# Layer A: the last rotated product of two query blocks side by side in halves of TensorE's rows

## The reference, cut to what matters

```
q = concat([q[..., :MLA_NOPE], apply_rope(q[..., MLA_NOPE:], cos, sin)])     # 128 + 64
k = concat([k[..., :MLA_NOPE], apply_rope(k[..., MLA_NOPE:], cos, sin)])     # 128 + 64
s = jnp.einsum('bqhd,bkhd->bhqk', q_blk, k).astype(jnp.float32) * scale
p = jax.nn.softmax(s, axis=-1)
o = jnp.einsum('bhqk,bkhd->bqhd', p, v)
```

## Time and profile before

| | |
|---|---|
| median of 3 runs | 1351.1 us (1350.52 to 1354.14) |
| the profiled execution, its own time | 1349.92 us |
| its span in the trace | 1348.1 us |
| PE busy | 1339.7 us, 99% of the span |
| PEld busy | 1163.8 us, 86% |
| DVE, ACT, POOL busy | 66%, 50%, 29% |
| granted TensorE clock | full in all slices |

### The profile page before, as it was taken

The page is one execution under the profiler, slowest core; times in us unless marked ns, Lnnn a source line. Parts: engine busy times, 40 slices in busy tenths (PEclk is TensorE's granted clock), DMA queues, the critical chain, the costliest instruction groups (busy, mean ns, idle before and its releaser), DMA issues.

```text
span 1348.1 us, 20503 instructions
## 1 busy us (share of the span) xinstructions
PE 1339.7 (99%) x7160; PEld 1163.8 (86%) x7160; DVE 890.7 (66%) x1811; ACT 678.0 (50%) x1544; POOL 395.3 (29%) x511
## 2 busy tenths in 40 slices
PE   9999999999999999999999999999999999999999
PEld 7889888888888889988888898888888888899887
DVE  6776688878796757888582524767766634267871
ACT  6554466545565546777451413545444323157760
POOL 0421251330011323846202213423300122337560
PEclk9999999999999999999999999999999999999999
DMA  8958745334779797541875545333144652654325
GB/s 313 333 211 287 254 145 172 129 137 136 253 240 397 264 360 264 201 151 47 319 259 189 180 157 181 106 110 95 49 150 155 203 174 80 217 178 151 103 75 187
DMA packets 111926, 256.59 MB, mean 190 GB/s; under 512 B 11344, under 2 KB 49104, under 8 KB 111824
## 3 DMA queue, kind: packets, MB, share of 16 engines
q1 hardware_dynamic: 106352, 247.58, 53.0%
q10 hardware_dynamic: 5472, 7.69, 1.8%
HBM read 167.15 MB, written 88.08 MB: 189 GB/s over the span
## 4 chain that ended last, share of the span: by engine, by line
PE 89%; DVE 4%; ACT 2%; DMA 2%; issue 1%; POOL 1%; SPq 0%; ACTq 0%; DVEq 0%; POOLq 0%
PE bank L2057 25%; PE bank L2059 25%; PE bank L2058 25%; PE bank L2102 8%; PE bank L2415 3%; PE bank L2063 2%; PE bank L2064 2%; DMA w_raw<-in_w_mem 1%; DVE w_split L1269 1%; ACT prob L886 1%; DVE probT L1281 1%; DMA w_raw<-in_w_a 0%; DMA w_split<-kept_w 0%; DVE prob L1789 0%; ACT w_split L849 0%
## 5 line engine op out<-in xcount | busy, mean ns | idle before, releaser
L2057 PE MATMUL bank<-actT,w_split 128*128 128x512 f32 x544 | 214.9, 395 | 0.0
L2059 PE MATMUL bank<-actT,w_split 128*128 128x512 f32 x544 | 212.2, 390 | 0.0
L1928 POOL TENSOR_TENSOR prob<-prob,rinv 128x256 f32<-128x256 f32 x192 | 131.0, 714 | 247.8 <-DVE rinv L1443 247.8
L1269 DVE TENSOR_TENSOR w_split<-w_raw,w_split 128x512 fp32r<-128x512 f32 (+3 forms) x204 | 142.0, 708 | 81.6 <-ACT w_split L849 78.9
L849 ACT ACTIVATE w_split<-w_raw 128x512 fp32r<-128x512 f32 (+3 forms) x204 | 122.3, 607 | 126.6 <-DMA kept_w<-w_split 57.8
L2057 PE MATMUL bank<-w_split,actT 128*128 128x512 f32 (+3 forms) x512 | 171.2, 334 | 0.8 <-DMA w_split<-kept_w 0.4
L2058 PE MATMUL bank<-w_split,actT 128*128 128x512 f32 (+3 forms) x512 | 170.2, 332 | 0.0
L2059 PE MATMUL bank<-w_split,actT 128*128 128x512 f32 (+3 forms) x512 | 170.2, 332 | 0.0
L2058 PE MATMUL bank<-actT,w_split 128*128 128x512 f32 x384 | 149.9, 390 | 0.0
L1281 DVE TENSOR_TENSOR probT<-bank,probT 128x512 fp32r<-128x512 f32 (+1 forms) x192 | 112.1, 639 | 21.7 <-ACT probT L859 19.5
L868 ACT ACTIVATE sq<-bank 128x512 f32<-128x512 f32 (+4 forms) x128 | 60.4, 480 | 129.9 <-PE bank L2059 123.1
(11 more groups left out here) (197 smaller groups left out, 3065.3 us busy)
## 6 DMA issues: line engine op xcount, KB each, us to landing
w_split<-kept_w SPq DMA_DIRECT2D x120, 512.0 KB, 4.0
kept_w<-w_split SPq DMA_DIRECT2D x104, 512.0 KB, 5.6
w_raw<-in_w_mem SPq DMA_DIRECT2D x64, 256.0 KB, 3.4
kept_w<-part_split SPq DMA_DIRECT2D x32, 512.0 KB, 5.0
part_split<-kept_w SPq DMA_DIRECT2D x30, 512.0 KB, 4.1
w_raw<-in_w_b SPq DMA_DIRECT2D x44, 256.0 KB, 5.0
w_raw<-in_w_out SPq DMA_DIRECT2D x38, 256.0 KB, 4.5
w_raw<-in_w_a SPq DMA_DIRECT2D x32, 256.0 KB, 4.7
```

Of the source, the lines that this page charges most:

```text
L1269: dve.tensor_tensor(halves(n)[1], w_raw[:, RAW_AT[n] % RAW, 0:width], halves(n)[0].bitcast(fp32), ALU.subtract).then_inc(w_lo_dve, 1)
L1928: pool.tensor_tensor(t, t, rinv[:, par, i:i + 1].to_broadcast(list(t.shape)), ALU.mult).then_inc(p_pool, 1)
L2057: nc.tensor.matmul(out, lhs[0], rhs[0], start=start, stop=False, skip_group_check=skip)
L2059: return nc.tensor.matmul(out, lhs[1], rhs[0], start=False, stop=stop, skip_group_check=skip)
```

## The change

`krT[:, 1, s, :]` now holds the lo part of the rotated key in both halves: DVE writes it twice, and the two memsets go. A new view `q_other[p]`, 256 columns of a row of `actT` that is unused at that time, gets from ACT the hi part of the rotated query of the odd blocks (1 and 3) for both heads of the pair, each in the half in which `qT` has the lo part. The second matmul of `mm2` is taken out of each block's five. Instead, behind the fourth matmul of block 1 and of block 3, two matmuls stand over 64 rows each: that of the block before, from `qT` and `krT` in `half(s)`, and that of the block itself, from `q_other` and `krT` in the other half. They write two different banks.

```diff
+        q_other = [actT[:, 2 * p + 1, 0:2 * P].rearrange("p (b n) -> p b n", b=2) for p in range(PAIRS)]
...
+            def odd_blocks(t):
+
+                return t.rearrange("p (i b n) -> p i b n", i=2, b=2)[:, :, 1, :]
...
                                 hi(("aT", L, p, 4), qT[half(j), 2, j, :], bank(("aT", L, p, 4))[half(j), :], first=j == 0)
+                                hi(("aT", L, p, 4), q_other[p][half(1 - j)], odd_blocks(bank(("aT", L, p, 4))[half(j), :]), first=False)
...
-                for s in range(2):
-                    dve.memset(krT[half(1 - s), 1, s, :].bitcast(fp32), 0.0)
...
                                 lo(("aT", L, p, 4), qT[half(1 - j), 2, j, :], bank(("aT", L, p, 4))[half(j), :],
-                                   qT[half(j), 2, j, :], last=j == 1)
-                                ins = lo(("aT", L, p, 5), krT[half(j), 1, j, :], bank(("aT", L, p, 5))[half(j), :],
-                                         krT[half(j), 0, j, :], last=j == 1, ahead=1)
+                                   qT[half(j), 2, j, :], last=j == 1, ahead=1)
                                 count("hi")
+                                lo(("aT", L, p, 5), krT[half(j), 1, j, :], bank(("aT", L, p, 5))[half(j), :],
+                                   krT[half(j), 0, j, :], last=False, ahead=1)
+                                ins = lo(("aT", L, p, 5), krT[half(1 - j), 1, j, :], bank(("aT", L, p, 5))[half(j), :],
+                                         krT[half(1 - j), 0, j, :], last=j == 1)
                                 if j == 0:
                                     ins.then_inc(first_head, 1)
...
                                 mm3(bank(use)[:], tuple(qT[:, s, a, i * P:(i + 1) * P] for a in range(2)),
                                     tuple(kT[:, a, s, :] for a in range(2)), True, False)
-                                mm2(bank(use)[:], qT[:, 2, s, i * P:(i + 1) * P],
-                                    tuple(krT[:, a, s, :] for a in range(2)), False).then_inc(full(use)[0], 1)
+                                nc.tensor.matmul(bank(use)[:], qT[:, 2, s, i * P:(i + 1) * P], krT[:, 0, s, :], start=False, stop=False)
+                                if i % 2 == 1:
+                                    before = ("aS", L, h, i - 1)
+                                    nc.tensor.matmul(bank(before)[:], qT[half(s), 2, s, (i - 1) * P:i * P], krT[half(s), 1, s, :],
+                                                     start=False, stop=True).then_inc(full(before)[0], 1)
+                                    nc.tensor.matmul(bank(use)[:], q_other[p][half(1 - s), i // 2, :], krT[half(1 - s), 1, s, :],
+                                                     start=False, stop=True).then_inc(full(use)[0], 1)
```

## The result

The changed kernel takes 1359.29 us (median of 5 runs, 1357.87 to 1361.6) where before took 1350.52 us beside it: ratio 1.0062, interval 1.005 to 1.0073. It is slower by 8.8 us by the medians and 8.4 by the ratio. I had forecast 1345.9 us, with 1358 as the end of the range.

What follows compares the result with a forecast made beforehand. The prediction took PE's queue of matmuls to bound the kernel: 5.7 us gained by 32 pairs, less 0.5 us of one softmax wait, takes 1351.1 to 1345.9 us, with a range of 1343.8 to 1358 us.

Steps and rivals of the forecast that it cites:

- What bounds the kernel: Whole kernel: PE, busy 99%, runs a queue of matmuls, so a cheaper matmul shortens the kernel by that much.
- The pair's own price: Layer A's 32 pairs: two overlapping products cost about 240 ns, for two weight loads, where they cost 454 before.
- The changes of rows: Borders of each pair, 128 to 64 rows and back: 35 ns for both changes, pair 275 ns, gain 5.7 us.
- the rival that I gave 0.25: Pair borders: array emptied at each change, up to 162 ns, 64 times; 1355.1 us; chance 0.25 for slower by over 0.3%.
- its form with exposed loads: Pair borders: weight load not hidden either, 118 ns more each change, pair 800 ns, 1362.7 us; chance 0.1 of the 0.25.
- `first_head`: First pair of each layer A: DVE's second key write still ends 0.26 us before PE's first scores load; no wait.
- The banks: Banks of the transposed tiles: PE comes to each over 1 us after it is read, added instructions counted; no wait.
- DVE becomes late: Layer A: DVE's added 11 us makes PE wait; 1 us in each of eight pairs; no chance worth a number.
- The softmax of the last pair: Last pair of the first layer A: DVE about 1.0 us late against 0.90 us of room; PE waits about 0.5 us once.
- The sum: Whole kernel: -5.7 for the pairs and +0.5 of waiting give -5.2 us, so 1345.9 us.

Runs made afterwards that it cites:

- 64 stays: Kernel before, with every block's second rotated product run alone over the 64 rows of half(s), where it stands: 1377.55 us against 1351.48, ratio 1.0197.
- the work alone: Changed kernel with its added DVE and ACT work, but PE's order of before, second products over 128 rows: 1353.79 us against 1350.6, ratio 1.0023.
- same_half: Changed kernel, but the odd block's product reads the same half of the rows as the pair's first: 1366.72 us, ratio 1.0119 to before.

## Why the prediction was wrong, step by step

**What bounds the kernel**: right. PE's products stand one behind the other, and what a pair costs more came through to the time: 26.1 us for 64 stays.

**The pair's own price**: right in direction, and better than forecast. I took 240 ns for two loads one behind the other. They start together (185.59 and 185.59), and inside a stay the pair is 227 ns plus 3. The Trainium skill's page TensorE: Matmul & The Clock Gate (Part 3: Packing small matmuls) says that matmuls in different row groups start about 4 ns apart; the trace agrees, with 3 or 4 ns in all 32 pairs. It also says that the load is pulled ahead. That doesn't carry over to the border of a stay: both loads wait for the change, 316 to 325 ns behind the start of the product before.

**The changes of rows**: this is the step that failed. I put 35 ns on the two changes of a pair, "nearer to the 6 ns of the only change that is shown than to the 162 of the end". They cost 404 by the trace and 408 by the time of 64 stays. The change to transposes that I took as the nearest row keeps all 128 rows; it says nothing on the array's division, and its loads stay hidden. What decides is the rival that I gave 0.25, in its form with exposed loads, which had 0.1 of that and which my range left out. Its terms were mis-sized, too: the emptying costs 91 to 96 ns and not 162, so the end of a product's record was no measure of it; the load costs 108 to 111, where I had 118; and the pair itself 230, where I had 240. With these it gives 230 + 404 = 634 ns for a pair, as measured, and not my 800. The Trainium skill's page TensorEngine Tiling (Array Packing), Key Properties, says that a change of mode drains TensorE. The trace agrees in that no load starts until the change is over, and shows that the load behind it is uncovered as well, which more than doubles the price.

**`first_head`**: I forecast no wait. PE waited 0.24 us in each layer A. I counted DVE's 0.69 against a room of 0.95, and left out that DVE's first write of the key waits for both of ACT's hi parts. `q_other` pushes these back: DVE waits 0.55 us for them before it adds its 0.69.

**The banks**: I forecast no wait, and looked only at the banks of the transposed tiles themselves. DVE takes its work in order, so its delay reached `q_st`, 15 us further on, whose banks had 0.95 and 0.37 us of room. In the work alone that costs 1.3 us at one place. The rival "DVE becomes late", which I gave no chance, holds 3.2 us with the work alone and 2.1 in the changed kernel.

**The softmax of the last pair**: forecast 0.5 us once, measured 0.6 us in the changed kernel. The size is right, but by luck. I had DVE 1.0 us late, since 0.31 of its 1.38 was to disappear in a wait for ACT. That wait grew instead, from 0.31 to 0.55 + 0.16, as in the run of the work alone:

```profile
311.94 1.38 DVE L1287 TENSOR_TENSOR krT<-bank,krT 64x512 fp32r<-64x512 f32 x2 [0.55 <-ACT krT L864]
...
314.20 1.40 DVE L1287 TENSOR_TENSOR krT<-bank,krT 64x512 fp32r<-64x512 f32 x2 [0.16 <-ACT krT L864]
```

So DVE was 1.8 us late, and in that run PE waits 1.0. In the changed kernel PE didn't come 0.3 to 0.4 us earlier, as I had it, but 0.4 later by two stays, and this hid part of it.

**The sum**: in the changed kernel's trace the pairs cost 5.7 us at their place and 0.4 in the products just behind them, which take 231 to 236 ns. The waits that can be named are 2.1 us (two of 0.24, then 0.4 and 0.5 at 200 us, 0.6 in the last pair). The span grew by 9.2; the other 1.0 us are differences at the start and in waits for weight tiles, which also go up and down by 0.2 to 1.2 us between the other runs. The price of the pairs alone, with the 0.5 us that I had for the softmax, would have given 1351.1 + 5.8 + 0.5 = 1357.4 us, just inside my range; the waits that I had left out took the time beyond its end.

## What to carry to other kernels

Products over half of the rows do run side by side and start within 3 or 4 ns of each other, but in a stream of full-row products each stay in halves costs about 400 ns, and a pair of 512 columns gives back 227. A stay of two such pairs came out even here; that more pairs would gain is my estimate from these two numbers, and no run shows it. When a row of the trace stands in for an unknown price, ask whether it has the same mechanism; a change of kind that keeps the array whole is no bound for one that divides it. And when work is added to an engine that works in order, follow its delay to every later bank that it frees, not only to the tiles of the change.

## What the runs showed of the hardware

The loads of two halves start within 3 or 4 ns of each other, while loads over all rows are 0.108 us or more apart in all but 8 of some 7,160 cases of the trace of before. Inside a stay a load in the same half is hidden under the running product, as outside. At a change into 64 rows no load starts until 316 to 325 ns behind the start of a product of 512 columns, 89 ns or more after its successor would have started, and at the change back it is the same, 317 to 323 ns (`same_half`). From a product to transposes nothing of this kind is seen, 233 ns and a load that starts 3 or 4 ns behind the product; nor on the way back, where the load starts 1 or 2 ns behind the last transpose.
